# A third Strassen pair in the branch projections of a merge stage

## What is computed

```python
merged = jax.nn.sigmoid(gate_a) * (y_a @ p_a) + jax.nn.sigmoid(gate_b) * (y_b @ p_b)
x = x + merged @ w_out
```

## Time and profile before

| | us |
|---|---|
| median of three runs | 1725.6 |
| lowest and highest | 1725.37, 1726.65 |
| the profiled execution's own time | 1725.04 |
| its span, first to last instruction | 1723.3 |
| merge stage's seven double blocks in it | 488.2 to 785.4 |

### The profile page before, as it was taken

The page is one execution under the profiler, slowest core; times in us unless marked ns, Lnnn a source line. Parts: engine busy times, 40 slices in busy tenths (PEclk is TensorE's granted clock), DMA queues, the critical chain, the costliest instruction groups (busy, mean ns, idle before and its releaser), DMA issues.

```text
span 1723.3 us, 25512 instructions
## 1 busy us (share of the span) xinstructions
PE 1717.2 (100%) x8652; PEld 1459.6 (85%) x8652; DVE 1306.4 (76%) x1805; ACT 987.8 (57%) x1329; POOL 9.9 (1%) x22
## 2 busy tenths in 40 slices
PE   9999999999999999999999999999999999999999
PEld 7888888888888888888888888888888888888887
DVE  6788876667788888887665667777777777799888
ACT  7765655657854444555654565555555555566454
POOL 0000000000000000000000000000000000000000
PEclk9999999999999999999999999999999999999999
DMA  8566565554456666666755456555555555665565
GB/s 326 185 173 183 171 170 174 173 174 149 159 181 196 198 196 205 207 195 221 291 193 186 147 171 192 182 192 189 186 190 186 189 189 186 203 203 188 199 210 178
DMA packets 90970, 331.06 MB, mean 192 GB/s; under 512 B 10224, under 2 KB 10480, under 8 KB 89872
## 3 DMA queue, kind: packets, MB, share of 16 engines
q1 hardware_dynamic: 89424, 321.96, 56.8%
q0 software_dynamic: 1472, 8.12, 2.6%
HBM read 326.83 MB, written 2.10 MB: 191 GB/s over the span
## 4 chain that ended last, share of the span: by engine, by line
PE 99%; DMA 0%; DVE 0%; SPq 0%; ACT 0%; issue 0%
PE ps L424 22%; PE ps L427 11%; PE ps L643 10%; PE ps L642 10%; PE ps L641 10%; PE ps L405 8%; PE ps L407 8%; PE ps L406 8%; PE ps L527 1%; PE ps L528 1%; PE ps L526 1%; PE ps L571 1%; PE ps L570 1%; PE ps L740 0%; PE ps L585 0%; PE ps L578 0%
## 5 line engine op out<-in xcount | busy, mean ns | idle before, releaser
L1493 DVE TENSOR_TENSOR w_lo<-w_raw,w_hi 128x1024 fp32r<-128x1024 f32 x486 | 589.7, 1223 | 307.4 <-ACT w_hi L914 306.4
L914 ACT ACTIVATE w_hi<-w_raw 128x1024 fp32r<-128x1024 f32 x486 | 507.8, 1056 | 370.4 <-PE ps L427 150.0
L424 PE MATMUL ps<-u,w_hi 128*128 128x512 f32 x1664 | 580.8, 395 | 0.0
L427 PE MATMUL ps<-u,w_lo 128*128 128x256 f32 x1664 | 461.8, 278 | 0.0
L424 PEld LDWEIGHTS ps<-u,w_hi 128*128 128x128 f32 x1664 | 312.1, 188 | 72.1
L427 PEld LDWEIGHTS ps<-u,w_lo 128*128 128x128 f32 x1664 | 312.7, 188 | 0.2
L405 PE MATMUL ps<-w_hi,u 128*128 128x512 f32 x416 | 166.1, 399 | 1.0 <-DVE w_lo L1525 1.0
L407 PE MATMUL ps<-w_hi,u 128*128 128x512 f32 x416 | 162.4, 390 | 0.0
L406 PE MATMUL ps<-w_lo,u 128*128 128x512 f32 x416 | 162.2, 390 | 0.0
L643 PE MATMUL ps<-w_hi,h_lo 128*128 128x512 f32 x256 | 99.6, 389 | 0.0
L405 PEld LDWEIGHTS ps<-w_hi,u 128*128 128x128 f32 x416 | 78.3, 188 | 17.1 <-DVE u L1520 1.4
(11 more groups left out here) (502 smaller groups left out, 2913.7 us busy)
## 6 DMA issues: line engine op xcount, KB each, us to landing
w_raw<-in_stream SPq DMA_DIRECT2D x600, 512.0 KB, 3.4
x_tok<-in_x SPq DMA_DIRECT2D x2, 1024.0 KB, 8.1
mem_raw<-in_mem_by_feature POOLq DMA_DIRECT2D x2, 1024.0 KB, 8.0
x_tok<-in_x POOLq DMA_DIRECT2D x2, 1024.0 KB, 8.9
mem_tok<-in_mem POOLq DMA_DIRECT2D x2, 1024.0 KB, 15.3
x_t<-in_x_t SPq DMA_DIRECT2D x7, 256.0 KB, 5.0
w_raw<-in_stream SPq DMA_DIRECT2D x4, 256.0 KB, 5.0
m_st<-ncm POOLq DMA_DIRECT2D x8, 128.0 KB, 6.4
```

The costliest lines, as they stand in the source:

```text
L424: pe.matmul(ps[:, bank + m, :], w_hi[:, s, lo:lo + P], act[:, kc, :, :].rearrange("p h t -> p (h t)"), start=(kc == 0), stop=False)
L427: mm = pe.matmul(ps[:, bank + m, T:2 * T], w_lo[:, s, lo:lo + P], act[:, kc, 0, :], start=False, stop=(kc == KC - 1))
L914: act.activation(w_hi[:, s, :], w_raw[:, s, :], ACT.Copy).then_inc(hi_made, 1)
L1493: TTo(w_lo[:, s, :], w_raw[:, s, :], w_hi[:, s, :].bitcast(F32), ALU.subtract).then_inc(lo_made, 1)
```

## The change

The blocks no longer share one list of Strassen pairs. Blocks 0 to 3 have them at p = 2, 4 and 6, blocks 4 to 6 at 3 and 6 as before: 18 in place of 14. There are eight forms in place of six: three for `y_a`, three for `y_b`, two for `u`. The four form slots `nm_*` are used again by forms 4 and 5, whose sums wait until block 1 has used the old content. The forms' turns in `FORM_AT` move to p = 1 and 3. On ScalarE form 0's high part comes ahead of the first turn's weights; on VectorE a form's low part comes at the head of the next turn, ahead of the weights and of the extra sums, and form 0's low part ahead of turn 0. The host packs the weights of the new Strassen pairs with the halves swapped, as it did for the old.

```diff
-MFAST = (3, 6)
-MSUMS = MBLOCKS * len(MFAST)
-MFORMS = 3 * len(MFAST)
+MFAST = ((2, 4, 6),) * 4 + ((3, 6),) * 3
+MFIRST = [sum(len(at) for at in MFAST[:b]) for b in range(MBLOCKS + 1)]
+MSUMS = MFIRST[MBLOCKS]
+MFORM = (0, 0, 3, 3, 6, 6, 6)
+MFORMS = 8
-FORM_AT = {(0, 2): 1, (1, 2): 2, (2, 2): 3, (3, 2): 4, (4, 2): 5}
+FORM_AT = {(0, 1): 1, (0, 3): 2, (1, 1): 3, (1, 3): 4, (2, 1): 5, (2, 3): 6, (3, 1): 7}
...
                     split(Pos(G_MERGE), 2 * n + 1)
-                if n == 0:
-                    merge_form_high(0)
...
-                if i == 4:
+                if i in (4, 5):
+                    dve.wait_ge(sem("fast_done"), MFIRST[1] + i - 3)
+                if i == 6:
                     dve.wait_ge(w_used, G_MERGE + 4 * KPB)
...
             merge_form_sums(0)
+            merge_form_low(0)
             for n in range(MBLOCKS * KPB):
                 b, p = n // KPB, n % KPB
-                if p == MFAST[-1]:
+                if (b, p - 1) in FORM_AT:
+                    merge_form_low(FORM_AT[b, p - 1])
+                if p == MFAST[b][-1]:
                     extra_sums(b, lambda c: m_bank(b + 1, c), um_sum)
...
-                if n == 0:
-                    merge_form_low(0)
                 if (b, p) in FORM_AT:
                     merge_form_sums(FORM_AT[b, p])
-                if (b, p - 1) in FORM_AT:
-                    merge_form_low(FORM_AT[b, p - 1])
```

More of the change, by code:

```diff
@@ L269, in m_form @@
         def m_form(i):
-            return (nm_hi[:, i, :], nm_sum[:, i, :], nm_lo[:, i, :]) if i < 4 else (
-                nu_hi[:, i - 4, :], nu_sum[:, i - 4, :], nu_lo[:, i - 4, :])
+            return (nm_hi[:, i % 4, :], nm_sum[:, i % 4, :], nm_lo[:, i % 4, :]) if i < 6 else (
+                nu_hi[:, i - 6, :], nu_sum[:, i - 6, :], nu_lo[:, i - 6, :])
         def m_fast(n):
             b, p = n // KPB, n % KPB
-            return len(MFAST) * b + MFAST.index(p) if b < MBLOCKS and p in MFAST else None
+            return MFIRST[b] + MFAST[b].index(p) if b < MBLOCKS and p in MFAST[b] else None
         def pair_slots(w, s):
@@ L693, in merge_fast @@
             def merge_fast(b, p):
-                i = len(MFAST) * (b // 2 if b < 4 else 2) + MFAST.index(p)
+                i = MFORM[b] + MFAST[b].index(p)
                 hi, raw, lo = m_form(i)
@@ L699, in merge_fast @@
                           lambda part: (hi[:, part], lo[:, part]), lambda m: (um_hi[:, m, :], um_lo[:, m, :]),
-                          lambda c: m_bank(b, c), lambda c: m_bank(b + 1, c), p == MFAST[0], p == MFAST[-1])
+                          lambda c: m_bank(b, c), lambda c: m_bank(b + 1, c), p == MFAST[b][0], p == MFAST[b][-1])
             for b in range(MBLOCKS):
@@ L710, in _ @@
                         merged_T(0)
-                    if p == MFAST[0] and b:
+                    if p == MFAST[b][0] and b:
                         pe.wait_ge(sem("mg_parts"), b)
-                    if p == MFAST[0] and b == MBLOCKS - 1:
+                    if p == MFAST[b][0] and b == MBLOCKS - 1:
                         pe.wait_ge(sem("mg_lo"), 2)
-                    if p in MFAST:
+                    if p in MFAST[b]:
                         merge_fast(b, p)
@@ L1252, in _ @@
                 b, p = n // KPB, n % KPB
-                if p == MFAST[-1]:
-                    act.wait_ge(sem("fast_done"), len(MFAST) * (b + 1))
+                if p == MFAST[b][-1]:
+                    act.wait_ge(sem("fast_done"), MFIRST[b + 1])
                     act.activation(um_sum[:, 0, :], ps[:, m_bank(b + 1, 0), :], ACT.Copy).then_inc(sem("extras_read"), 1)
+                if n == 0:
+                    merge_form_high(0)
                 if m_fast(n + 2) is not None:
@@ L1925, in merge_form_sums @@
             def merge_form_sums(i):
-                q = MFAST[i % 2]
-                act_t = (y_a, y_b, u)[i // 2]
+                act_t, b = ((y_a, 0), (y_b, 2), (u, 4))[i // 3]
+                q = MFAST[b][i - MFORM[b]]
                 hi, dst, lo = m_form(i)
@@ L1986, in _ @@
                     g = G_MERGE + 2 * (n + 2)
-                    if p + 2 == MFAST[0] and b:
+                    if p + 2 == MFAST[b][0] and b:
                         dve.wait_ge(sem("mg_parts"), b)
@@ L2324, in lay_out, with double @@
     p_a, p_b, w_out = (np.asarray(i[n])[0] for n in ("p_a", "p_b", "w_out"))
-    def double(w, n0, v, m0):
+    def double(b, w, n0, v, m0):
         both = np.concatenate([w[:, n0:n0 + BLK], v[:, m0:m0 + BLK]], 1)
@@ L2329, in double @@
             pair = both[2 * p * P:(2 * p + 2) * P].reshape(2, P, 1024).copy()
-            if p in MFAST:
+            if p in MFAST[b]:
                 pair[0] = np.roll(pair[0], BLK, axis=1)
             chunks.append(pair)
-    for w in (p_a, p_b):
-        for n in (0, 2):
-            double(w, n * BLK, w, (n + 1) * BLK)
+    for b in range(4):
+        w, n = (p_a, p_b)[b // 2], 2 * (b % 2)
+        double(b, w, n * BLK, w, (n + 1) * BLK)
     for n in range(3):
-        double(w_in, gb0 + n * BLK, w_in, ga0 + (n + 1) * BLK)
+        double(4 + n, w_in, gb0 + n * BLK, w_in, ga0 + (n + 1) * BLK)
     block(w_in, gb0 + 3 * BLK)
```

## The result

The changed kernel takes 1731.35 us (median of seven runs, 1730.48 to 1731.98); the kernel before, in the same sets of runs, 1725.34. The ratio is 1.0033, 95% interval 1.0021 to 1.0045: slower by 6.0 us. The span of the profiled execution grew from 1723.3 to 1729.8 us. The ratios in this document leave out one execution, of a later kernel (two more pairs), that took 2886 us at a mean granted clock of 0.556.

A forecast was written before the change was run, and what follows sets the result against it. PE was taken as the bound, with DVE too slow in turns holding a form. Saving 2.4 us and stalling 8.1 gives +5.7: 1725.04 becomes 1730.7, median 0.6 above, 1731.3; own range 1729.5 to 1733, chance 0.70.

The forecast's parts named there:

- The gain: Blocks 0 to 3: one more Strassen pair each takes 0.61 us off PE, 2.44 us in all, if operands are in time.
- The turn of 12.16 against 10.27 us: Between Strassen preparations with a form between, DVE needs 6.72 + 2.27 + 3.17 = 12.16 us, PE 10.27.
- The stops, place by place: PE stalls before pairs 4 and 6 of blocks 0 to 2 and pair 4 of block 3, together 8.1 us.
- The steady ones: PE stalls before pair 6 of blocks 0, 1 and 2, 1.89 us each.
- those of pair 4 in blocks 1 and 2: PE stalls before pair 4: 0.20 us in block 1, 0.58 us in block 2.
- rival B: Heads of blocks 1 to 3: raw weights land late, 0.3 to 0.8 us more each, 1732.2 to 1733.7; chance 0.12.
- Should be gone: Sign: DVE's row "um_sum waits for the stream" should vanish in blocks 0 to 3, with idle time there near zero.
- the single buffer of the operand sums: DVE cannot work ahead, since this buffer is free only when PE has ended the Strassen pair before.
- A: DVE's load over a block, 41.6 us, is just under PE's 41.7, so not slower: 1723.2 or 1724.3; chance 0.10.
- C: PE's clock falls for the stalls; 20 us at half clock add 10 us: 1741; chance 0.03, shared with other losses.

The follow-up runs named there:

- the run with one form: The changed kernel with blocks 0 to 3 all using form 0, so forms 1 to 5 are never made and results are wrong: 1722.55 us, ratio 0.9985.
- less of it: The changed kernel with a form's sums between its turn's two splits and its low part behind the second: 1726.43 us, ratio 1.0008 to the kernel before.
- more of it: The changed kernel with the first sum (0.72 us) of forms 1 to 7 made twice, 1738.75 us, or three times, 1743.7 us.
- the same order where there is air: The kernel before, its Strassen pairs and form turns kept, with only the new places of the low part and form 0: 1725.25 us, ratio 1.0001.
- the run with two more pairs: Against the kernel before, one more Strassen pair in blocks 1 and 3 only, forms spread out, sums between a turn's splits: 1724.12 us, ratio 0.9993.

## Why the prediction was right

**The size.** 1731.3 was forecast, 1731.35 measured. That it agrees to a tenth is luck: the rise was put at 5.7 us and is 6.0 by the medians (6.5 by the profiled executions), and the kernel before, taken at 1725.6 in the sum, has a median of 1725.34 in the larger set.

**The gain.** 4 x 0.61 = 2.44 us was right: 2.4 us by the run with one form.

**The turn of 12.16 against 10.27 us.** The trace has 12.16 to the digit, the 0.70 us wait for ScalarE in it. That DVE's forms and their wait are the cause, and not a companion, was shown in four ways: less of it (1726.43), none of it (1722.55), more of it (1738.75, 1743.7), and the same order where there is air (1725.25).

**The stops, place by place.** Expected 1.43, 1.89, 0.20, 1.89, 0.58, 1.89, 0.20, together 8.1 us. By the starts around each stop on PE they are 1.33, 1.82, 0.51, 1.82, 0.92 (0.24 of it at the head of block 2), 1.83 and 0.17, together 8.4; by block lengths 8.8, as other steps are wider by hundredths of a microsecond. The steady ones were right: from stop to stop PE takes 522.50 - 510.34 = 12.16 us, which is DVE's turn, where the run with one form has 514.34 - 504.05 = 10.29. The terms that were too small are those of pair 4 in blocks 1 and 2, by 0.3 us each. What they lacked was rival B: the first preparation of a block still waits for the stream, here on DVE in block 1.

```profile
536.19 2.35 DVE L1495 TENSOR_TENSOR w_lo<-w_raw,w_hi 128x1024 fp32r<-128x1024 f32 x2
538.85 1.22 DVE L1889 TENSOR_TENSOR um_sum<-w_raw 128x1024 f32<-128x1024 f32 x1 [0.31 <-DMA w_raw<-in_stream]
...
576.32 2.36 DVE L1495 TENSOR_TENSOR w_lo<-w_raw,w_hi 128x1024 fp32r<-128x1024 f32 x2
```

The 4.5 us of work in front of it nearly covers the landing: 0.31 us is left, and 0.28 in block 2, where the heads of blocks 1 and 3 in the earlier trace rows had 1.9 and 2.4. The stop at block 2's head is DVE's too: the first low part for that block (the last line, first of two, ready at 576.32 + 1.22 = 577.54) stands behind the gating and the extra sums, and PE starts at 577.70. It hurts nothing more, since pair 4 is late by DVE's sum in any case. "Should be gone" was wrong, "0.3 to 0.8 us in each block" was right at its lower end for two of three. Most of what the profiled execution's 6.5 us has over my 5.7 is this excess; the median of the seven runs lies lower.

**An argument that was not needed.** The prediction held the single buffer of the operand sums to be what keeps DVE from working ahead. In the tight turns of the changed kernel DVE never waits for that buffer: no row there waits for PE. It is simply full: in block 1, 42.0 us of work and 1.7 us of waits (two for ScalarE, one for the stream) in 44.4 us, where PE's own work is 41.7. The buffer binds only where DVE is ahead, as in the run with one form (0.61 and 1.21 us), and there it costs nothing. Nor does the buffer keep DVE from handing a lead on, as block 3 of the run with two more pairs shows. A second buffer was not tried.

**The rivals.** A (the load over a block decides, 1723.2 to 1724.3) fell: over a block DVE's work does just about fit, and yet 2 to 3 us are lost in each of blocks 0 to 2. What A left out is the waits. Whether the single turn or the whole block, counted with its waits, is the right unit is not shown: in block 1 DVE waits for nothing of PE's, so both sums give the same. C (the clock) did not come in: 1.00 in all four stretches with stops of 1.8 us. The small chance that I gave it was right for this kernel only; with 0.7 us more in each gap it came, at 0.9 to 1.6 us a fall and not the 10 us of that rival.

## What to carry to other kernels

Before work is moved off the bounding engine at the price of more on a helper, add up the helper's work and its waits between two of its deadlines, with the lead that it brings, not its share over the whole kernel: 76% busy was no room here, since the new work came in turns of 12.2 us against 10.3, one behind the other. In such turns a helper's wait for another engine's answer (0.7 us for ScalarE) is paid in full; putting independent work between question and answer gave 4.9 of the 6.0 us back. And make what is used by several blocks (the forms) in the blocks that have no extra work of their own.

## What the runs showed of the hardware

PE's granted clock fell to half (1.2 GHz) for about 3 us with gaps of 2.2 us, start to start, in two of three cases and of 2.97 us in three of three, and not with the gaps of 1.5 us in the changed kernel, nor with one of 2.46 us. The falls cost 1.3 and 1.6 us at the 2.2 us gaps and 0.9 at the longer ones, where the clock was already low before PE resumed. So where the clock falls, a helper that is late by two microseconds or more costs a third to four fifths more than its lateness. Beside that, a stop of PE costs about 0.16 us more than the idle time shown, and 0.1 us on the matmul behind it.
